# One of eight opening transfers issued by ScalarE after a warm-up product, and three high parts made on VectorE

## What is computed

```python
def rmsnorm(x, g):
    xf = x.astype(jnp.float32)
    y = xf * lax.rsqrt(jnp.mean(xf * xf, axis=-1, keepdims=True) + EPS)
    return (y * g.astype(jnp.float32)).astype(x.dtype)

def swiglu_ffn(x, w_in, w_out):
    gate, up = jnp.split(x @ w_in, 2, axis=-1)
    return (jax.nn.silu(gate) * up) @ w_out

def reference(x, ...):
    for l in range(L):
        x = x + 0.5 * swiglu_ffn(rmsnorm(x, norm_ffn1[l]), w_ffn1_in[l], w_ffn1_out[l])
        ...
        x = x + merged @ w_out[l]
        x = x + 0.5 * swiglu_ffn(rmsnorm(x, norm_ffn2[l]), w_ffn2_in[l], w_ffn2_out[l])
    return rmsnorm(x, norm_final)
```

## Time and profile before

| | us |
|---|---|
| median of 3 runs | 1126.44 |
| lowest to highest | 1126.33 to 1127.19 |
| the profiled execution's own time | 1126.32 |
| its span (first to last instruction in the trace) | 1124.5 |
| outside its span | 1.8 |

### The profile page before, as it was taken

How to read it: one execution, slowest core, us unless ns; L and a number is a source line. 1 busy time by engine, 2 the same in 40 slices (tenths; PEclk the granted TensorE clock), 3 DMA queues, 4 the chain that set the end, 5 groups by cost and what they waited for, 6 DMA issues and landing times.

```text
span 1124.5 us, 13052 instructions
## 1 busy us (share of the span) xinstructions
PE 1116.8 (99%) x5005; PEld 924.0 (82%) x5005; DVE 801.8 (71%) x986; ACT 649.3 (58%) x742; POOL 39.0 (3%) x67
## 2 busy tenths in 40 slices
PE   9999999999999999999999999999999999999998
PEld 6888888888888888888888888888888888888886
DVE  6756566899998875655476655378999987665553
ACT  7755546664647765554475554376637477756441
POOL 0000000000200100000000000000002001000000
PEclk9999999999999999999999999999999999999999
DMA  9986665863756686656597666467638667866541
GB/s 362 325 257 207 217 237 180 264 205 128 266 201 195 212 291 210 210 200 224 147 313 235 210 201 227 170 219 246 199 122 275 230 193 230 268 218 224 159 187 38
DMA packets 129710, 244.65 MB, mean 218 GB/s; under 512 B 98912, under 2 KB 99296, under 8 KB 105072
## 3 DMA queue, kind: packets, MB, share of 16 engines
q1 hardware_dynamic: 127296, 237.01, 63.7%
q0 software_dynamic: 1648, 6.06, 1.5%
q10 hardware_dynamic: 704, 0.75, 0.2%
HBM read 219.16 MB, written 1.05 MB: 196 GB/s over the span
## 4 chain that ended last, share of the span: by engine, by line
PE 96%; DVE 1%; DMA 1%; ACT 1%; issue 0%; POOL 0%; SPq 0%; POOLq 0%; DVEq 0%; ACTq 0%
PE acc L423 31%; PE acc L425 31%; PE acc L424 31%; DMA retT_planes<-ret_planes 1%; PE acc L467 1%; PE acc L472 1%; PE acc L476 1%; DMA first<-in_first 1%; DVE w_lo L1250 0%; PE tr L610 0%; PE tr L517 0%; ACT w_hi L821 0%; PE tr L602 0%; PE ret L622 0%; PE ret L624 0%
## 5 line engine op out<-in xcount | busy, mean ns | idle before, releaser
L1250 DVE TENSOR_TENSOR w_lo<-raw,w_hi 128x2048 fp32r<-128x2048 f32 (+2 forms) x204 | 445.4, 2213 | 84.2 <-ACT w_hi L821 83.9
L821 ACT CAST w_hi<-raw 128x2048 fp32r<-128x2048 f32 (+2 forms) x204 | 375.2, 1849 | 216.1 <-PE acc L425 207.2
L423 PE MATMUL acc<-w_hi,xT_hi 128*128 128x512 f32 x1152 | 450.9, 391 | 0.2 <-DVE w_lo L1250 0.2
L425 PE MATMUL acc<-w_hi,xT_lo 128*128 128x512 f32 x1152 | 448.4, 389 | 0.0
L424 PE MATMUL acc<-w_lo,xT_hi 128*128 128x512 f32 x1152 | 448.3, 389 | 0.0
L425 PEld LDWEIGHTS acc<-w_hi,xT_lo 128*128 128x128 f32 x1152 | 216.2, 188 | 45.5
L423 PEld LDWEIGHTS acc<-w_hi,xT_hi 128*128 128x128 f32 x1152 | 216.3, 188 | 45.3 <-DVE w_lo L1250 0.9
L424 PEld LDWEIGHTS acc<-w_lo,xT_hi 128*128 128x128 f32 x1152 | 216.3, 188 | 43.9
L1333 DVE SCALAR_TENSOR_TENSOR h<-acc,rs,silu_gate 128x256 f32<-128x256 f32 x88 | 42.5, 483 | 153.8 <-ACT silu_gate L888 153.5
L424 PE MATMUL acc<-w_lo,hT_hi 128*128 128x512 f32 x348 | 135.4, 389 | 0.0
L423 PE MATMUL acc<-w_hi,hT_hi 128*128 128x512 f32 x348 | 135.4, 389 | 0.0
(11 more groups left out here) (146 smaller groups left out, 638.2 us busy)
## 6 DMA issues: line engine op xcount, KB each, us to landing
raw<-in_weights SPq DMA_DIRECT2D x192, 1024.0 KB, 5.0
raw<-in_weights SPq DMA_DIRECT2D x8, 512.0 KB, 3.5
raw<-in_weights SPq DMA_DIRECT2D x12, 256.0 KB, 7.9
bias<-in_gate_bias POOLq DMA_DIRECT2D x6, 512.0 KB, 6.6
first<-in_first SPq DMA_DIRECT2D x7, 384.0 KB, 6.6
x<-in_x SPq DMA_DIRECT2D x2, 512.0 KB, 12.2
scale_row<-in_pool_scale POOLq DMA_DIRECT2D x2, 512.0 KB, 7.0
hT_planes<-h_planes SPq DMA_TRANSPOSE x54, 3.0
```

Source lines behind the costliest of these rows:

```text
L423: nc.tensor.matmul(o, a_hi, b_hi, start=first, stop=False)
L425: return nc.tensor.matmul(o, a_lo, b_hi, start=False, stop=last)
L821: nc.scalar.copy(w_hi[:, hf % HIGHS, 0:n], raw[:, hf % RAWS, 0:n]).then_inc(hi_split, 1)
L1250: nc.vector.tensor_tensor(w_lo[:, hf % RAWS, 0:n], raw[:, hf % RAWS, 0:n], w_hi[:, hf % HIGHS, 0:n].bitcast(F32), ALU.subtract).then_inc(l ...
```

## The change

Three edits. SP no longer issues slice 2 among its opening transfers; ScalarE does, as its first work behind the table load, and waits before it for a new semaphore `warmed`, which the sixth of TensorE's nine constant products raises. VectorE makes `xT_hi` of slices 0, 1 and 2 instead of slice 0 alone, and ScalarE leaves those of 1 and 2 out. TensorE waits for `first_x_hi` at each of the first three slices, where it waited for it at slice 0.

```diff
+DVE_HIGH = 3
+SIXTH = 5
...
+        warmed = sem("warmed")
...
                     for k in range(KT):
                         w_high, w_low = weights(2 * g + k // 4, k % 4 * NB, NB)
-                        if g == k == 0:
-                            pe.wait_ge(first_x_hi, 1)
+                        if g == 0 and k < DVE_HIGH:
+                            pe.wait_ge(first_x_hi, k + 1)
                         pe.wait_ge(first_hi, KT * g + k + 1)
...
-                for _ in range(n):
-                    nc.tensor.matmul(ret[:, 0, :], one.broadcast_to([P, P]),
-                                     one.broadcast_to([P, NB]), start=True, stop=True)
+                for i in range(n):
+                    mm = nc.tensor.matmul(ret[:, 0, :], one.broadcast_to([P, P]),
+                                          one.broadcast_to([P, NB]), start=True, stop=True)
+                    if i == SIXTH:
+                        mm.then_inc(warmed, 1)
...
-            for k in range(KT):
+            for k in (0, 1, 3, 4, 5, 6, 7):
                 load_step(sp, k)
...
             nc.scalar.preload_act_table_set("silu_and_others")
+            act.wait_ge(warmed, 1)
+            load_step(act, 2)
...
             cast_first(0)
             for k in range(1, KT):
-                first_x_high(k)
+                if k >= DVE_HIGH:
+                    first_x_high(k)
                 cast_first(k)
...
             def first_x_low(k):
-                if k == 0:
+                if k < DVE_HIGH:
 
                     dve.wait_ge(first_landed[k], 16)
                     nc.vector.tensor_scalar(xT_hi[:, k, :], first_x(k), first_gain(k), None,
                                             ALU.mult).then_inc(first_x_hi, 1)
-                    dve.wait_ge(first_x_hi, 1)
+                    dve.wait_ge(first_x_hi, k + 1)
                 else:
```

## The result

| | before | changed |
|---|---|---|
| median, us | 1126.46 (6 runs) | 1131.76 (6 runs) |
| lowest to highest | 1125.99 to 1127.19 | 1131.54 to 1132.80 |
| profiled span | 1124.5 | 1129.7 |

The changed kernel is slower by 5.30 us: ratio 1.0052, 95% interval 1.0041 to 1.0063 (the two medians alone give 1.0047, which lies inside). The prediction was 1126.05 with a range up to 1127.8; it was wrong in size and in sign. Nearly all of the loss arises in the first 17 us.

A forecast was written before the change was run, and what follows sets the result against it. TensorE was taken to bound the kernel. Slice 2 landing at 7.30 plus 0.70 puts its product at 8.00 instead of 8.39, other costs 0 or hidden: minus 0.39 from 1126.44 gives 1126.05 us, range 1125.3 to 1127.8.

The forecast's parts named there:

- The bound: Whole kernel: TensorE, busy 1116.8 of 1124.5 us; what is won or lost before 8.39 us moves the rest equally.
- a loss nobody planned: Opening: at most some 0.7 us to win, so the question of sign is mostly one of an unplanned loss.
- VectorE's high parts: Slices 0 to 2: slice 2's product 0.70 us behind its landing instead of 1.09, winning 0.39; VectorE's extra work costs 0.
- ScalarE's issue: Opening: slice 2 issued at 3.50 us, taking 0.44; first copy up to 0.05 later, hidden by slice 2's wait.
- When slice 2 lands: Slice 2's transfer on ScalarE's queue: bounded between 6.9 and 8.3 us, taken as 7.30, its earlier landing.
- The late end: Slice 2's latest landing, 8.3 us, if slices 2 and 3 go by turns from 4.5 us at the old pace.
- rival C: Slice 2 on ScalarE's queue starts late like `par`, landing at 11.3: plus 3.6 us, 1130.0; half-way 1128.2; chance 0.06.
- The slow stretch: Data movement from 5.3 to 6.7 us at 230 GB/s, between stretches of 380 and 396; some may not recur.
- the early end: Slice 2's earliest landing, 6.9 us, from slice 0's 3.2 us on empty queues and shared data engines.
- Slice 3 behind slice 2: Slice 3 lands at 8.3 us, can start at 9.4 at the latest, wanted at 9.4: cost 0, just hidden.

The follow-up runs named there:

- e4_sync_holds: The changed kernel with SP also waiting for the sixth constant product before issuing slice 3, so only slices 0 and 1 go ahead; 1126.67 us, ratio 1.0006.
- e5_third_product: The changed kernel with ScalarE issuing slice 2 behind the third constant product instead of the sixth; 1129.52 us, ratio 1.0026.
- e3_no_wait: The changed kernel without ScalarE's wait for the sixth product, so slice 2 is issued at once, at 0.78 us; 1127.83 us, ratio 1.0013.
- e7_filled_wait: The changed kernel with 16 more constant products on TensorE ahead of its wait for slice 2; 1129.74 us, ratio 1.0030.
- e6: The changed kernel with SP waiting for the sixth product before slice 5, so four transfers are ahead of slice 2; 1130.62 us, ratio 1.0039.
- e2: The changed kernel with VectorE making only slice 0's high part, as before, so only the transfer's move is left; 1132.02 us, ratio 1.0055.
- e10: The changed kernel with ScalarE issuing slice 2 behind the ninth constant product instead of the sixth; 1132.75 us from 2 runs, ratio 1.0061.
- e12_vector_only_again: The changed kernel with slice 2 back on SP's queue, leaving only VectorE's three high parts, measured again with more rounds; 1125.83 us, ratio 0.9998.
- e8: The changed kernel with slice 7 instead of slice 2 on ScalarE's queue, and slices 0 to 6 on SP's; 1126.21 us, ratio 1.0001.
- e9: The changed kernel with SP loading each of slices 3 to 7 as two transfers of smaller rows; 1128.33 us, ratio 1.0027.

## Why the prediction was wrong

**The bound.** Right. TensorE's opening sets the rest, and a change there goes through to the end undiminished: 5.07 us in the opening, 5.2 in the span. The sentence that sign was mostly a matter of a loss nobody planned was right as well; its weight was not.

**VectorE's high parts.** The mechanism was right. The term was mis-sized: from landing to product I took 0.70; it was 0.79 in the changed kernel (11.16 to 11.95) and 0.79 in e4_sync_holds (8.06 to 8.85), at the upper end that I had given, since the step from copy to product was 0.14 again and not 0.04, so the gain is 0.30 and not 0.39. Its cost at slices 1 and 2 was 0, as said.

**ScalarE's issue.** Right: at 3.53 us for 0.38, and the first copy at 3.98, 0.03 later than in the earlier trace rows, as slice 0's landing was.

**When slice 2 lands.** This is the step that failed. I bounded the landing by 6.9 and 8.3 and took 7.30, "the landing that slice 2 had"; it was 11.16. Both bounds rested on the same unspoken idea, that packets go by turns from the moment the second queue has any. They do go by turns once both move, but before q10's first packet the data engines moved more of SP's, on average each 20.3, 20.8, 21.6 and 23.6 in four kernels, with four, eight and six transfers ahead and with whole or split rows, counted from 1 us behind the issue (14.3 in e5_third_product, where the count fails). At this load 21 packets of 3 KB are 3.1 us. And the turns were not even at first: in the changed kernel, from 7.6 to 9.6 us,

```profile
q1 hardware_dynamic: 182, 0.50, 62.7%
q10 hardware_dynamic: 106, 0.32, 40.4%
```

The late end had a second fault: it counted only slices 0 to 3, where SP had issued slices 4, 5 and 6 too by then. The row that would have given the landing stood in the trace before, SP's own transfer issued at 3.55 us, landing at 11.20. The Trainium skill (DMA: Bandwidth & Descriptors, "Queues, rings and completion order") says that an engine takes the queues with work in turn, packet by packet, and that such a packet typically holds some 9 to 17 descriptors, the single pieces of a transfer. The runs agree on the turns once q10 has begun (133 against 138 packets of the profile in e3_no_wait). Whether the 20 or so that go ahead of the first turn have to do with the size of such a packet, no run here shows.

The trace also had `par`, a transfer of ScalarE's beside a loaded SP queue, which took 7.8 us for 160 KB; slice 2 took 7.6. (It was not the only one: `ident`, issued right behind it, took 7.5 us.) I had it as rival C, computed a landing of 11.3 from it, 0.14 off, and gave it 0.06, on the ground that `par` met larger packets and a transpose. That ground was a reason for caution, not for a price four microseconds lower: slice 0's landing, on empty queues, was a row of another kind. But that C came so near in its landing was partly luck. `par`'s first packet moved at 49.27, 2.35 us behind its issue, and 5.4 us went by in moving it; slice 2's moved 4.14 behind its issue, and the landing came 3.5 later.

**The slow stretch.** I leaned to the early end because the stretches beside the slow one ran at 380 and 396 GB/s. That was misread: the one directly ahead of it, 4.4 to 5.3 us, has 290, and the data engines were not busy all through, with a share of 0.81 in the slow stretch itself.

**Rival C's price.** It gave 1130.0 for a landing at 11.3. The measured 1131.76 is 1.8 more, of which 1.51 are the half-rate products behind the wait; no part of the prediction had asked what a wait of 3.8 us does to TensorE's clock. e7_filled_wait shows that cost by itself. It is not a fixed one: 1.5 us in the traces of the changed kernel, e5 and e6, 2.3 in those of e2 and e10.

**Slice 3 behind slice 2.** That slice 3 was just hidden was right: once slice 2 came early (e12_vector_only_again), slice 3's landing at 8.30 set the next wait. It also means that the most to be won by slice 2 alone was never 0.7 us in every execution. And the 7.30 itself was one draw: 6.50 and 6.38 in the two executions with the same transfers in the same order. Why the transfers slow down between 5.3 and 6.7 us stays open.

## What to carry to other kernels

A transfer that is put on a second queue late hardly jumps the first queue: here it landed about when one issued on the loaded queue at the same moment would have, 11.16 against 11.20 us. So its price must be read from such a transfer, never from the first one of the program. If an urgent transfer has to overtake, issue less ahead of it (e4_sync_holds), or issue it first, and then look at whom it delays (e3_no_wait). Where a change can lengthen a wait of TensorE in a program that it bounds, price the wait twice, once for itself and once for the products behind it. And in a program's first microseconds read TensorE's pace from the distance of its starts, since the clock column may stand on no record.

## What the runs showed of the hardware

- With six to eight of SP's transfers issued before it, the first ScalarE packet moved 3.5 to 4.2 us behind its issue (3.53 in e8, 4.19 in e7, 4.14 in the changed kernel); with four ahead 3.90 (e6), 2.93 (e5) and, with the rows split, 2.62 (e9); with two ahead 1.84 (e4), with one being issued at the same time 1.73 (e3). SP's first packets of the program moved 1.0 behind theirs. Why ScalarE's queue starts 0.8 later even with little ahead is open.
- From 1 us behind the issue to that first packet, the data engines moved 20 to 24 of SP's packets each, on average, in seven kernels, whether of 3072 bytes (0.90 to 0.96 MB in all) or of 1024 and 2048 (0.54 MB); in e5_third_product 14.
- ScalarE's transfer landed close to its place in the order of issue over both queues in nine kernels (largest distance 0.4 us), and at least 0.7 us ahead of it in e10_ninth_product.
- After TensorE had waited 3.85 us, its products ran at half rate at first and the granted clock read 0.61 over the stretch of 4.41, against 1.00 where constant products filled the wait; a cost of 1.5 us by the trace and 1.8 by the medians. Waits of 2.15 and 3.18 us (e5, e6) had the same behind them, waits of 4.28 and 3.65 us (e2, e10) a cost of 2.3; waits of 0.67, 0.7 and 1.92 us (before, e4, e9) were followed by products at the usual distance.
- The opening's constant products ran at half the pace of the same ones later (2.72 us for six against 1.48), under a clock column of 1.00 for which the trace has no record.
